# Five ring slots for weights and three for their high parts in a two-block transformer kernel, instead of four and four

## The reference, cut to what matters

```python
def modulate(x, shift, scale): ...
c_act = jax.nn.silu(c)
shift, scale, gate = jnp.split(c_act @ mod_w[layer] + mod_b[layer], 3, axis=-1)
h = modulate(rmsnorm(x, norm_g[layer]), shift, scale)
x = x + gate[:, None, :] * out
```

## Time and profile before

| what | before |
|---|---|
| median of 3 runs | 3064.54 us |
| lowest and highest | 3064.34, 3067.28 us |
| the profiled execution | 3066.89 us |
| its span in the profile | 3065.1 us |
| PE busy | 3016.8 us, 98% of the span |
| VectorE, ScalarE, GpSimd busy | 72%, 48%, 12% |
| HBM read | 699.96 MB, 234 GB/s over the span with what is written |
| chain that ended last, by engine | PE 90%, DVE 4%, DMA 2%, ACT 2%, issue 1% |

### The profile page before, as it was taken

The page is one execution under the profiler, slowest core; times in us unless marked ns, Lnnn a source line. Parts: engine busy times, 40 slices in busy tenths (PEclk is TensorE's granted clock), DMA queues, the critical chain, the costliest instruction groups (busy, mean ns, idle before and its releaser), DMA issues.

```text
span 3065.1 us, 46429 instructions
## 1 busy us (share of the span) xinstructions
PE 3016.8 (98%) x16676; PEld 2553.0 (83%) x16676; DVE 2205.7 (72%) x2677; ACT 1483.0 (48%) x2001; POOL 358.6 (12%) x397
## 2 busy tenths in 40 slices
PE   8999999999999999999999999899999999999998
PEld 8888888888888888888888888799888888888887
DVE  6779887667767766886766765899875657566665
ACT  6455444454444345444444443656554544555553
POOL 0000000025555431550000000000000000000000
PEclk9999999999999999999999999999999999999999
DMA  7667776658888876998888985555555578544445
GB/s 249 217 234 282 248 277 220 197 185 310 306 282 315 309 268 183 302 301 254 287 285 256 267 278 192 159 200 197 179 189 185 181 274 309 197 153 151 151 165 192
DMA packets 272833, 719.25 MB, mean 235 GB/s; under 512 B 27456, under 2 KB 120128, under 8 KB 271360
## 3 DMA queue, kind: packets, MB, share of 16 engines
q1 hardware_dynamic: 251616, 669.28, 65.2%
q10 hardware_dynamic: 13936, 28.69, 2.9%
q0 software_dynamic: 7088, 18.62, 1.7%
HBM read 699.96 MB, written 16.53 MB: 234 GB/s over the span
## 4 chain that ended last, share of the span: by engine, by line
PE 90%; DVE 4%; DMA 2%; ACT 2%; issue 1%; ACTq 0%; SPq 0%; DVEq 0%
PE psum L881 60%; PE psum L818 11%; PE psum L862 6%; PE psum L821 5%; DMA ring<-in_stream 2%; DVE ring_parts L2527 1%; PE psum L920 1%; PE psum L933 1%; PE psum L999 1%; PE psum L1138 1%; ACT hi_parts L1496 1%; PE psum L1289 1%; PE psum L841 0%; PE psum L1007 0%; PE psum L947 0%
## 5 line engine op out<-in xcount | busy, mean ns | idle before, releaser
L2527 DVE TENSOR_TENSOR ring_parts<-ring,hi_parts 128x1024 fp32r<-128x1024 f32 x1000 | 1220.2, 1251 | 404.8 <-ACT hi_parts L1496 399.6
L1496 ACT ACTIVATE hi_parts<-ring 128x1024 fp32r<-128x1024 f32 x1000 | 1025.3, 1057 | 769.5 <-DMA ring<-in_stream 740.7
L881 PE MATMUL psum<-hi_parts,arena_low_parts 128*128 128x512 f32 x3440 | 1100.9, 391 | 4.3 <-DVE ring_parts L2527 4.2
L881 PEld LDWEIGHTS psum<-hi_parts,arena_low_parts 128*128 128x128 f32 x3440 | 645.9, 188 | 142.9 <-issue 5.3
L881 PE MATMUL psum<-hi_parts,arena_high_parts 128*128 128x512 f32 x2224 | 731.4, 394 | 1.1 <-DVE arena_high_parts L2252 1.1
L881 PE MATMUL psum<-ring_parts,arena_low_parts 128*128 128x512 f32 x1872 | 728.9, 389 | 0.0
L881 PEld LDWEIGHTS psum<-hi_parts,arena_high_parts 128*128 128x128 f32 x2224 | 418.1, 188 | 90.5 <-issue 3.9
L881 PEld LDWEIGHTS psum<-ring_parts,arena_low_parts 128*128 128x128 f32 x1872 | 351.7, 188 | 71.3
L881 PE MATMUL psum<-ring_parts,arena_high_parts 128*128 128x512 f32 x960 | 374.1, 390 | 0.0
L818 PE MATMUL psum<-arena_low_parts,hi_parts 128*128 128x512 f32 x992 | 321.0, 399 | 2.7 <-DVE ring_parts L2527 2.7
L862 PE MATMUL psum<-arena_low_parts,hi_parts 128*128 128x256 f32 (+1 forms) x1184 | 232.4, 287 | 2.1 <-DVE ring_parts L2527 1.4
(11 more groups left out here) (418 smaller groups left out, 2682.9 us busy)
## 6 DMA issues: line engine op xcount, KB each, us to landing
ring<-in_stream SPq DMA_DIRECT2D x1272, 512.0 KB, 4.6
ssm_kept<-work POOLq DMA_DIRECT2D x16, 512.0 KB, 6.8
arena_high<-ssm_kept ACTq DMA_DIRECT2D x11, 512.0 KB, 4.4
frac_kept<-work POOLq DMA_DIRECT2D x15, 256.0 KB, 6.0
early<-frac_kept ACTq DMA_DIRECT2D x15, 256.0 KB, 2.7
work<-ssm_kept ACTq DMA_DIRECT2D x5, 512.0 KB, 4.4
arena_high<-in_mem ACTq DMA_DIRECT2D x8, 256.0 KB, 7.1
arena_high<-in_x ACTq DMA_DIRECT2D x1, 2048.0 KB, 13.0
```

The source lines that it names most:

```text
L881: mm = pe.matmul(stream_bank(b + t), r32(x[part][:, kg * KG + kk, t * P:(t + 1) * P]), r32(cols), start=(kg == 0 and kk == 0 and n == 0), ...
L1496: act.activation(r32(hi[:, g % RING, cols]), ring[:, g % RING, cols], ACT.Copy).then_inc(hi_made, 1)
L2527: dve.tensor_tensor(r32(slot), slot, as32(hi[:, g % RING, cols]), ALU.subtract).then_inc(cut_done, 1)
```

## The change

`RING` becomes 5 and `hi` gets a ring of its own with `HI_RING` = 3 slots; together they take the same 64 KB of each partition. `HI[g]` is the count of split units up to entry g, and `SPLIT` is the new list of their places in `PLAN`. The slot in `hi` is now counted in split units, so that modulation and compression tiles take none. SyncE's conditions are written in terms of `RING` and follow by themselves; ScalarE's copy waits for the release of the third split unit before. The stream is padded to a multiple of 5 (635) in place of a multiple of 4 (636).

```diff
-RING, UNIT = 4, 2048
+RING, HI_RING, UNIT = 5, 3, 2048
...
+SPLIT = [_g for _g, _x in enumerate(PLAN) if _x[0] == "unit" and _x[1] != "cw"]
...
-        hi = two_types("hi", [P, RING, UNIT])
+        hi = two_types("hi", [P, HI_RING, UNIT])
...
+        def slot_of(w, g):
+
+            return w[:, (HI[g] - 1) % HI_RING if w is hi else g % RING, :]
...
-                return g % RING
+                return g
...
-                            mm = pe.matmul(bank, r32(hi[:, slot, cols]), both_parts(x, kk), start=(kk == first_ks[0]),
+                            mm = pe.matmul(bank, r32(slot_of(hi, slot)[:, cols]), both_parts(x, kk), start=(kk == first_ks[0]),
...
-                    if g >= RING:
-
-                        value = 2 * (g - RING) + h + 1
+                    if HI[g] > HI_RING:
+
+                        value = 2 * SPLIT[HI[g] - 1 - HI_RING] + h + 1
                         act.wait_ge(units_done, value if i is None else i * (2 * per) + value)
...
-                    act.activation(r32(hi[:, g % RING, cols]), ring[:, g % RING, cols], ACT.Copy).then_inc(hi_made, 1)
+                    act.activation(r32(slot_of(hi, g)[:, cols]), ring[:, g % RING, cols], ACT.Copy).then_inc(hi_made, 1)
...
-                        dve.tensor_tensor(r32(slot), slot, as32(hi[:, g % RING, cols]), ALU.subtract).then_inc(cut_done, 1)
+                        dve.tensor_tensor(r32(slot), slot, as32(slot_of(hi, g)[:, cols]), ALU.subtract).then_inc(cut_done, 1)
```

More of the change, by code:

```diff
@@ L626, in program @@
         few = {"idx_w": early[:, 0:S], "ngate": work[:, TMP[2], 0:S]}
+        def slot_of(w, g):
+            return w[:, (HI[g] - 1) % HI_RING if w is hi else g % RING, :]
         def ik_parts(of, g, h):
-            cols = of[:, g % RING, h * HALF:(h + 1) * HALF].rearrange("p (k n) -> p k n", n=P)
+            cols = slot_of(of, g)[:, h * HALF:(h + 1) * HALF].rearrange("p (k n) -> p k n", n=P)
             return cols[:, :, 0:64], cols[:, :, 64:64 + N_IDX]
@@ L817, in wide_unit @@
                         if form == "wide":
-                            mm = pe.matmul(bank, r32(hi[:, slot, cols]), both_parts(x, kk), start=(kk == first_ks[0]),
+                            mm = pe.matmul(bank, r32(slot_of(hi, slot)[:, cols]), both_parts(x, kk), start=(kk == first_ks[0]),
                                            stop=(kk == KT - 1))
                         else:
-                            mm = pe.matmul(bank[:, 0:S], r32(ring[:, slot, cols]), r32(x[0][:, kk, :]), start=False, stop=False)
+                            mm = pe.matmul(bank[:, 0:S], r32(slot_of(ring, slot)[:, cols]), r32(x[0][:, kk, :]), start=False, stop=False)
                     if all(j // (KT // 2) != h for j in first_ks[n + 1:]):
@@ L840, in first_wide_pair @@
                             for n, (w, moving, bank) in enumerate(order):
-                                mm = pe.matmul(bank, r32(w[:, slots[u], cols]), moving, start=(k == 0 and n == 0),
+                                mm = pe.matmul(bank, r32(slot_of(w, slots[u])[:, cols]), moving, start=(k == 0 and n == 0),
                                                stop=(k == KT - 1 and n == 1))
@@ L861, in t_unit @@
                         for n, (w, part) in enumerate(((hi, 0), (hi, 1), (ring, 0))):
-                            mm = pe.matmul(bank[0:m, half:half + S], r32(w[:, slot, cols]), r32(x[part][:, k, :]),
+                            mm = pe.matmul(bank[0:m, half:half + S], r32(slot_of(w, slot)[:, cols]), r32(x[part][:, k, :]),
                                            start=(k == 0 and n == 0), stop=(k == KT - 1 and n == 2))
@@ L877, in n_unit @@
                             for n, (part, w) in enumerate(((0, hi), (0, ring), (1, hi))):
-                                cols = w[:, slot, kk * CHUNK:(kk + 1) * CHUNK]
+                                cols = slot_of(w, slot)[:, kk * CHUNK:(kk + 1) * CHUNK]
                                 if phase in ("ff0", "ff1"):
-                                    cols = w[:, slot, h * HALF:(h + 1) * HALF].rearrange("p (a k n) -> p k a n", a=4, k=2)[:, kk % 2]
+                                    cols = slot_of(w, slot)[:, h * HALF:(h + 1) * HALF].rearrange("p (a k n) -> p k a n", a=4, k=2)[:, kk % 2]
                                 mm = pe.matmul(stream_bank(b + t), r32(x[part][:, kg * KG + kk, t * P:(t + 1) * P]),
@@ L897, in first_pair @@
                                 pe.wait_ge(*x1_turned(t, u))
-                            halves_of_tiles = [w[:, slot, h * HALF:(h + 1) * HALF].rearrange("p (a k n) -> p k a n", a=4, k=2)
+                            halves_of_tiles = [slot_of(w, slot)[:, h * HALF:(h + 1) * HALF].rearrange("p (a k n) -> p k a n", a=4, k=2)
                                                for w in (hi, ring)]
@@ L920, in last_pair @@
                                     mm = pe.matmul(stream_bank(b + t), r32(x[part][:, kg * KG + kk, t * P:(t + 1) * P]),
-                                                   r32(w[:, slot, cols]), start=False,
+                                                   r32(slot_of(w, slot)[:, cols]), start=False,
                                                    stop=(kg == groups - 1 and kk == KG - 1 and n == 2))
```

## The result

| what | before | after |
|---|---|---|
| median, with 15 runs of each in one comparison | 3064.64 us | 3071.8 us |
| lowest and highest | 3062.13, 3068.03 us | 3068.42, 3073.42 us |
| ratio, 95% interval | | 1.0021, 1.0015 to 1.0028 |
| the profiled execution and its span | 3066.89, 3065.1 us | 3072.5, 3070.7 us |

The change costs 7.2 us in medians and 5.6 us between the two profiled executions. 3070.5 was forecast. Of the runs of the kernel before that stand beside the second set of experiments one took 14235.17 us, and its ratios leave it out.

What follows compares the result with a forecast made beforehand. PE was taken as the bound, busy 3016.8 of 3065.1 us. Waits at three phase ends +11.2, fifth slot -6.0 and clock +0.8 sum to +6.0, giving 3070.5 us on the median of 3064.54; range 3064.0 to 3077.0.

Steps and rivals of the forecast that it cites:

- End of fo1, so and wo: Phase ends: second-unit copies wait for the last-but-one unit's late release, delaying urgent work; +4.7, +4.3, +2.2, together +11.2 us.
- Fifth weight slot: Weight ring: units issued one slot earlier, landings up to 3.6 us earlier, removing late-landing gaps; -6.0 us, bounds -6.4 and 0.
- seven gaps counted as late landings: PE's five gaps at L881 and two at L818, 5.3 us, worth up to 6.4, taken as removable by a deeper ring.
- All five gaps of L881 are of this kind: Claim that all 4.2 us of PE's L881 gaps for ring parts came from late landings; two stood in the rows.
- Plain stretches, the stricter wait: Stretches without modulation tiles: ScalarE's copy starts about 1 us later, covered since PE needs the unit two units later; 0.
- Clock at wo: After wo's new 2.2 us gap, a stretch at 1.2 GHz may follow; between 0 and +1.7, taken as +0.8 us.
- Startup: Kernel start: SyncE may issue ten halves instead of eight before the first release; 0, upper bound +1 us.
- tail: End of stream: two fewer 512 KB padding copies ahead of the output's issue on SyncE; 0 to -0.3 us.
- A: Rival: the fifth slot gives nothing, DMA being nearly full, so waits and clock alone count; 3076.5 us, chance 0.14.
- B: Rival: the waits at the three phase ends are covered and only the deeper ring pays; 3058.5 us, chance 0.09.
- C: Rival: both halves of the argument are too large, or so's or wo's wait is covered; 3066.5 us, chance 0.12.
- D: Rival: the change does not do what it says, and neither wait ever ended last; 3064.5 us, chance 0.05.

Runs made afterwards that it cites:

- experiment 5: Kernel before, four and four slots, with only the copies for unit 1 of ff0, su and kvt waiting as with three high slots: 3077.27 us, ratio 1.0044.
- experiments 6 to 8: Changed kernel with the next phase's second-unit copy and cut behind the first tile's chain at one end each: wo 3068.72, fo1 3067.06, so 3067.6 us.
- experiment 2: Changed kernel with the fifth weight slot taken back, so four ring slots and three high slots: 3076.62 us, ratio 1.0037.
- experiment 4: Kernel before, four and four slots, with the next phase's second-unit copy and cut put behind the first token tile's chain: 3064.26 us, ratio 0.9997.
- experiment 1: Changed kernel with the next phase's second-unit copy and cut behind the first token tile's chain at all three ends: 3060.65 us, ratio 0.9986.
- experiments 3: Changed kernel with four ring and four high slots, keeping only the counting of high slots in split units: 3064.7 us, ratio 1.0000.

## Why the prediction was right

*End of fo1, so and wo (forecast 4.7 + 4.3 + 2.2 = 11.2).* The table of stretches gives 4.65, 4.22 and 2.14, in all 11.01; experiment 5 has the waits alone, experiments 6 to 8 each alone. ScalarE idles for PE's L925 as was said, but 5.74 us, and ahead of the first half's copy, which waits for the same late unit; the second half follows after 0.30. I had followed the second half alone. The gap before su was forecast as one of 11.5 us; it is two, 5.43 at L1278 and 6.60 at L938, because the short matmuls between are delayed too. The sum came out, the picture of it was too simple. That the two parts miss each other by so little is partly luck.

*Fifth weight slot (forecast -6.0, bounds -6.4 and 0).* The stretches between the ends gave 6.04 us by the table and 5.5 with the clock's part taken out. By medians it is 4.8 (experiment 2 less after), again 4.8 (experiment 5's 11.95 above its kernel before, less the 7.16 of after) or 3.6 (experiment 4 less 1, with no wait in the way), each known to 2 us or so. So the slot is worth some 3.6 to 5.5 us, and the term was too large by 0.5 to 2.4. Its working was partly wrong. Of the seven gaps counted as late landings, one never was: PE's wait in kvn, 0.98 us before 2513.67 in the kernel before, is still there after, and longer. Its row before, and then three rows after:

```profile
2513.67 0.50 PE L881 MATMUL psum<-hi_parts,arena_low_parts 128*128 128x512 f32 x1 [0.98 <-DVE ring_parts L2527]
```

```profile
2513.25 1.09 ACT L1479 ACTIVATE arena_high<-psum 128x512 f32<-128x512 f32 x2 [2.68 <-PE psum L886]
...
2515.32 1.23 DVE L2197 TENSOR_TENSOR arena_high_parts<-arena_high,arena_high_parts 128x1024 fp32r<-128x1024 f32 x1 [3.49 <-ACT arena_high_parts L1427]
...
2520.12 0.50 PE L886 MATMUL psum<-hi_parts,arena_low_parts 128*128 128x512 f32 x1 [1.31 <-DVE ring_parts L2532]
```

Read backwards: PE waits for a cut that stands behind L2197 on VectorE; L2197 waits for ScalarE, and ScalarE for PE's last matmul of a bank. The wait is one of order, and the deeper ring did not take it: it is 1.3 us in all five profiles with five slots. Another of the seven, the one of 0.66 us at L818, fell only to 0.38. And the gap of 1.43 us before 1317.58 was a late landing only at one remove, as these rows of the kernel before show:

```profile
1312.16 4.14 DVE L2539 SCALAR_TENSOR_TENSOR early<-ring,c_act,early 128x1024 f32<-128x1024 f32 x2
...
1313.35 1.07 ACT L1496 ACTIVATE hi_parts<-ring 128x1024 fp32r<-128x1024 f32 x1 [2.89 <-DMA ring<-in_stream]
```

The high part was ready at 1314.42, but VectorE stood in its two products for a modulation tile until 1316.22, having come late to them from a cut that waited for an earlier landing. "All five gaps of L881 are of this kind" was the step that failed; I had looked at two of them and taken the others with them. What made up for it is the delay that leaves no gap, found in experiment 2: the gaps at L881 and L818 fell by 2.9 and 0.7 us, 3.6 in all, and the stretches gave 5.5. That the two errors nearly cancel is luck.

Nor is any single gap of one profile a fixed thing. The one of 1.43 us is gone in experiments 3 and 4 too, which have four slots, and others stand elsewhere. Only the sum at this line tells the sizes apart: 4.2, 4.7, 3.6 and 4.3 us in the four kernels with four and four slots, one gap of 1.3 us in all five with five and three, and 2.0 us with four and three.

*Plain stretches, the stricter wait (forecast 0).* Seen in 121 waits of ScalarE for L886, 170.3 us in all and 2.8 at most, with no gap of PE for a ring part at a place where before had none. The cover was there: PE needs the unit two units later. Experiments 2 and 5, with three high slots everywhere and with the three waits alone, say the same with 3076.62 and 3077.27.

*Clock at wo (forecast +0.8 of 0 to 1.7).* Absent in the profiled execution of after, where PEclk is 1.00, and present in that of experiment 5, where it cost 0.36 us and not 1.7. So the upper bound was too high: the price of a slow stretch was taken from its length alone, and at wo PE had a wait for VectorE to hide it in. The term was 0.4 to 0.8 too large. By the Trainium skill (TensorE: Matmul & The Clock Gate, Part 1) the number of slow matmuls varies between runs of one kernel. The two profiles are of two kernels and only fit this; the single runs of the kernel before in the second set bear it out for one kernel: with a mean granted clock of 0.997, 0.996 and 0.995 they took 3062.1, 3064.3 and 3066.0 us on average (4, 12 and 10 runs).

*Startup (0, bound +1) and tail (0 to -0.3).* PE reached the matmul near 445 0.63 us later. The matmul that started at 23.18 in the kernel before had it already. It is not the fifth slot: in experiment 4, with four slots, that matmul starts later still. Here is its row in the kernel after and then in experiment 4:

```profile
23.89 0.39 PE L867 MATMUL psum<-arena_low_parts,hi_parts 128*128 128x256 f32 x1 [0.27 <-DVE ring_parts L2532]
```

```profile
24.12 0.39 PE L863 MATMUL psum<-arena_low_parts,hi_parts 128*128 128x256 f32 x1 [0.27 <-DVE ring_parts L2531]
```

The tail cannot be told from the rest of its stretch.

*A number of the working.* The waits of PE for L2527 are not 9.4 us in all but 11.5: one of 2.1 us at L933, at 12.97 us while the kernel starts, was left out. It is 2.0 after, so nothing hangs on it.

*The sum.* +6.0 was forecast and +7.2 measured. The waits were right to 0.2 us; the slot's gain was put too high and the clock's price too high, and these two errors have opposite signs. That the forecast lies within 1.3 us owes something to this.

*The rivals.* A, the ring gives nothing: falls, experiment 2 is 4.8 us above after. B, the waits are covered and the ring pays: falls for this change; experiment 1 is what it described, and came to 3060.65 where B said 3058.5. C and D: the waits reached PE at all three ends in nearly the size that was forecast, and each part alone moves the time.

## What to carry to other kernels

When a ring of buffers is made shorter, look not at the steady state, where the wait for a free slot may be covered for 170 us, but at the places where the consumer releases a slot late (here a last pair that is run tile by tile) and an in-order engine has urgent work queued behind the instruction that waits. What counts is by how much the urgent chain behind it is delayed, 2.1 to 4.7 us here, and not the idle row of the engine that waits, 5.74 each time. Moving the non-urgent copy behind the urgent chain takes the delay away without a byte of memory: 11 us here, against the 3.6 to 4.8 that the deeper ring brings by medians. Of every gap that a change is to remove, follow the releaser back one step further before counting it, and look whether it stands in a second profile.

## What was not expected of the hardware

PE's recorded idle time is less than what late weights cost. At wo a gap of 2.14 us moved the next start by 2.30, since the row of the matmul before it reaches past the next start by some 0.16. Between after and experiment 2 the gaps for ring parts differ by 1.3 us and the spans by 3.8, of which some 2 are late starts that show no gap and 0.7 are the clock's.

The granted clock fell behind a gap of 2.14 us in one execution and not in another whose gaps around it are the same to 0.1 us. Behind the gaps of 1.54 and 0.60 us near 2965 us it fell in six of ten profiled executions.

What such a slow stretch costs depends on what PE waits for next: 1.6 us near 2970 us, 0.36 us at wo, for about the same length at 1.2 GHz.
